# Summing a normalised input's squares on GpSimd, between the weight splits, instead of on VectorE

## The reference

```python
def rms_norm(x, g):
    xf = x.astype(jnp.float32)
    y = xf * lax.rsqrt(jnp.mean(xf * xf, axis=-1, keepdims=True) + EPS)
    return (y * g.astype(jnp.float32)).astype(x.dtype)
...
        y = swiglu_2(rms_norm(x, ffn1_pre_g[l]), ffn1_w_gate[l], ffn1_w_up[l], ffn1_w_down[l])
        x = x + 0.5 * rms_norm(y, ffn1_post_g[l])
        y = hybrid_mixer(rms_norm(x, mix_pre_g[l]), w_in[l], cmp_pe[l], cmp_w1[l], cmp_w2[l],
                         nsa_out_g[l], ret_gn_g[l], w_out[l])
        x = x + rms_norm(y, mix_post_g[l])
```

## Time and profile before

| | |
|---|---|
| median of 3 runs (range) | 3390.71 us (3387.91 to 3391.46) |
| profiled execution | 3393.15 us, of which 3391.7 us span |
| mean granted TensorE clock | 0.985 of full speed |
| busy share PE / DVE / ACT / Pool | 97% / 38% / 37% / 40% |

### The profile page before, as it was taken

The page is one execution under the profiler, slowest core; times in us unless marked ns, Lnnn a source line. Parts: engine busy times, 40 slices in busy tenths (PEclk is TensorE's granted clock), DMA queues, the critical chain, the costliest instruction groups (busy, mean ns, idle before and its releaser), DMA issues.

```text
span 3391.7 us, 45793 instructions
## 1 busy us (share of the span) xinstructions
PE 3281.8 (97%) x17988; PEld 2783.1 (82%) x17988; DVE 1297.6 (38%) x2495; ACT 1242.9 (37%) x2333; POOL 1357.5 (40%) x897
## 2 busy tenths in 40 slices
PE   8999999999999999999999999999999999999998
PEld 6887788898888878888788888888977888688887
DVE  5465443215330534544353305331234553344311
ACT  4454332223222344553332223222334554333221
POOL 3452344444444432343244443444342243244442
PEclk9999999999999999999999999999999999999999
DMA  3221232322232231122123222322241122123322
GB/s 139 75 75 44 68 98 95 101 93 88 96 100 91 90 110 51 63 81 71 61 75 100 97 93 73 108 94 99 85 137 51 46 77 78 50 75 100 100 93 69
DMA packets 81236, 287.32 MB, mean 85 GB/s; under 512 B 8960, under 2 KB 11392, under 8 KB 80640
## 3 DMA queue, kind: packets, MB, share of 16 engines
q1 hardware_dynamic: 79584, 278.42, 25.2%
q10 hardware_dynamic: 1440, 5.98, 0.5%
HBM read 282.26 MB, written 2.10 MB: 84 GB/s over the span
## 4 chain that ended last, share of the span: by engine, by line
PE 85%; DVE 8%; ACT 4%; issue 2%; POOL 1%; DMA 1%; ACTq 0%; DVEq 0%; POOLq 0%
PE bank L263 23%; PE bank L265 22%; PE bank L264 22%; PE bank L1260 3%; PE bank L271 2%; PE bank L273 2%; PE bank L272 2%; PE bank L1236 2%; PE bank L1247 2%; ACT hhi L883 2%; DVE hlo L838 2%; DVE tmp L862 1%; POOL wlo L257 1%; DVE x L833 1%; PE bank L2993 1%
## 5 line engine op out<-in xcount | busy, mean ns | idle before, releaser
L257 POOL TENSOR_TENSOR wlo<-raw,whi 128x256 fp32r<-128x256 f32 (+2 forms) x838 | 1301.1, 1569 | 1880.7 <-ACT whi L243 1838.3
L263 PE MATMUL bank<-hhi,whi 128*128 128x512 f32 x2160 | 868.4, 402 | 10.1 <-POOL wlo L257 3.0
L264 PE MATMUL bank<-hlo,whi 128*128 128x512 f32 x2190 | 860.1, 393 | 0.0
L265 PE MATMUL bank<-hhi,wlo 128*128 128x512 f32 x2160 | 849.1, 393 | 0.0
L243 ACT ACTIVATE whi<-raw 128x1024 fp32r<-128x1024 f32 (+1 forms) x528 | 527.4, 1034 | 389.1 <-PE bank L265 299.5
L263 PEld LDWEIGHTS bank<-hhi,whi 128*128 128x128 f32 x2160 | 410.8, 190 | 96.9 <-issue 15.1
L264 PEld LDWEIGHTS bank<-hlo,whi 128*128 128x128 f32 x2190 | 416.6, 190 | 82.8 <-issue 1.0
L265 PEld LDWEIGHTS bank<-hhi,wlo 128*128 128x128 f32 x2160 | 409.9, 190 | 87.9
L263 PE MATMUL bank<-ff_ahi,whi 128*128 128x512 f32 x660 | 256.7, 389 | 0.0
L265 PE MATMUL bank<-ff_ahi,wlo 128*128 128x512 f32 x660 | 256.7, 389 | 0.0
L264 PE MATMUL bank<-ff_alo,whi 128*128 128x512 f32 x630 | 245.1, 389 | 0.0
(11 more groups left out here) (409 smaller groups left out, 5666.7 us busy)
## 6 DMA issues: line engine op xcount, KB each, us to landing
raw<-wstream SPq DMA_DIRECT2D x516, 512.0 KB, 3.7
raw<-wstream SPq DMA_DIRECT2D x20, 256.0 KB, 3.1
x<-xT ACTq DMA_DIRECT2D x4, 512.0 KB, 10.3
xa_v<-memT ACTq DMA_DIRECT2D x2, 1024.0 KB, 4.8
outT<-x SPq DMA_DIRECT2D x4, 512.0 KB, 2.8
consts<-consts ACTq DMA_DIRECT2D x1, 1062.0 KB, 15.3
m_lw<-lru_w ACTq DMA_DIRECT2D x1, 544.0 KB, 3.6
par<-par SPq DMA_DIRECT2D x2, 248.0 KB, 11.3
```

Source lines behind the costliest of these rows:

```text
L257: last = g.tensor_tensor(h.lo[:, o:o + step], h.raw[:, o:o + step], h.hi[:, o:o + step].bitcast(F32), ALU.subtract)
L263: t.matmul(out, l[0], r[0], start=start, stop=False)
L264: t.matmul(out, l[0], r[1], start=False, stop=False)
L265: return t.matmul(out, l[1], r[0], start=False, stop=stop)
```

## The change

Entry.dve loses its loop of seven adds. Entry.pool gets them: three behind the low part of (first + 1, half 1), four behind the low part of (first + 2, half 0), which is in four pieces, and ahead of root.pool. The waits, the order of the adds, the tiles and the operation stay as they are. Nothing changes on ACT, PE or SP.

```diff
@@ Entry.dve
-        acc = k.tmp[2]
-        for n in range(1, KT):
-            v.wait_ge(*self.sq[n])
-            if n >= 2:
-                v.wait_ge(*self.sq_added[n - 2])
-            v.tensor_tensor(acc[:, :], acc[:, :], self.sq_tile(n)[:, :], ALU.add).then_inc(self.sq_added.sem)
         self.root.dve()
@@ Entry.pool
         weight_lo(self.k, self.first + 1, 1, pieces=4)
+        self.add_squares(1, 4)
         weight_lo(self.k, self.first + 2, 0, pieces=4)
+        self.add_squares(4, KT)
         self.root.pool()
+
+    def add_squares(self, n0, n1):
+        g, acc = self.k.nc.gpsimd, self.k.tmp[2]
+        for n in range(n0, n1):
+            g.wait_ge(*self.sq[n])
+            if n >= 2:
+                g.wait_ge(*self.sq_added[n - 2])
+            g.tensor_tensor(acc[:, :], acc[:, :], self.sq_tile(n)[:, :], ALU.add).then_inc(self.sq_added.sem)
```

## The result

| | median of the runs | lowest to highest | ratio to before (95%) |
|---|---|---|---|
| before | 3389.68 us (4 runs) | 3387.91 to 3391.46 | |
| after | 3420.34 us (4 runs) | 3417.03 to 3423.57 | 1.009 (1.0073 to 1.0108) |

The change makes the kernel 30.7 us slower. The forecast was 3422 us, with a range of 3406 to 3432. The profiled execution took 3418.72 us with a span of 3417.1 us, 25.4 us above the profiled one of before.

What follows compares the result with a forecast made beforehand. PE, busy 97% of the span, bounds the kernel, so its waits for the adds count. Seven "post" Entries 27.3, the "final" 2.4 and clock 1.5 sum to 31.2 us: 3422 us predicted, range 3406 to 3432.

Steps and rivals of the forecast that it cites:

- The add on Pool: One 128x512 add on Pool: 1.27 us, with 0.1 between adds a pitch of 1.37; bounds 0.72 and 1.45.
- The gain of the pieces: Pool's four low-part pieces, without DVE's adds in between, take 2.8 us instead of 4.16, a gain of 1.4 us.
- DVE's delay d: Pool's first three adds hold up DVE's chain in the second half of the tokens: 2.0 us, bounds 0 and 3.6.
- Per "post" Entry: PE's restart after the adds: 1.9 + 2.0 = 3.9 us later, seven times, 27.3 us.
- The "final" Entry: The eighth Entry: Pool's adds end at 780.8, 2.4 us later than PE comes; DVE's delay is hidden there.
- Behind the restart: Order after the last add moves as a whole; only PE's clock may change, 1.5 us for two Entries.
- the sum: All terms for the whole kernel: 27.3 + 2.4 + 1.5 = 31.2 us slower.
- A (no contention): Rival: Pool's first three adds cost DVE nothing; 15.7 us slower, or 3406 us; chance 0.12.
- B (heavier contention): Rival: DVE's delay near 3.6 us, or pitch 1.5, and clock low in each Entry; 44 us, 3435; chance 0.13.
- its third part: The heavier-contention rival's claim that PE's clock is low in each Entry, 3 us of its 44.
- C (a cheap add): Rival: adds cheap on Pool, so the chain's end stays or comes earlier; 3387 us; faster 0.03, no change 0.04.
- D: Rival: PE doesn't wait longer, because its wait is for something other than the adds; chance 0.01.

Runs made afterwards that it cites:

- the first try: Kernel before (adds on DVE), PE's means four steps into the third chunk, row ten in, Pool's second low part ahead of root.pool: 3393.68 us, ratio 1.0014.

## Why the prediction was right

**The add on Pool.** Taken as 1.27 us from the slope of two widths; measured 1.267 in the median. The four of the tail with their gaps: 5.4 us forecast, 5.47 measured.

**The gain of the pieces.** 2.8 us forecast, 2.81 measured.

**DVE's delay d.** 0.4, 1.5 and 2.0 us forecast after each Pool add; 0.4 after the first (low ends at 1143.14 instead of 1139.33 + 3.41), 1.48 after the second and 1.85 at the pieces. Where it costs is made plain by the two kernels with the parts apart. With the first three adds on Pool alone it costs nothing, since four adds are left behind it on DVE instead of seven; it counts where Pool's longer tail stands behind it.

**Per "post" Entry.** 3.9 us forecast, 3.8 measured in the Entry shown, as 6.21 - 4.15 = 2.06 us more waiting at line 396 and 1.75 us of a longer second half. In five of the other six it is 3.8 as well; in the one whose wait had been 4.5 it is 3.4.

**The "final" Entry.** 2.4 us forecast; PE's wait there is 2.42 us, and its restart moves by 2.6 us from where the two kernels stood ahead of the Entry.

**Behind the restart.** 1.5 us had been set aside for the clock in two Entries. It was mis-sized: by ACT's copy of the row behind each restart, the eight Entries lose 5.8 us there. The two that had been named lose the most, 1.8 and 1.5 us, but four others lose 0.5 to 0.8 each. The last Entry, before and after:

```profile
3031.86 1.05 PE L396 MATMUL bank<-consts,tmp 128*128 128x1 f32 x8 [4.15 <-DVE tmp L862]
3038.98 0.60 ACT L897 ACTIVATE row<-bank 128x512 f32<-128x512 f32 x1 [8.29 <-PE bank L730]
```

```profile
3055.84 1.86 PE L396 MATMUL bank<-consts,tmp 128*128 128x1 f32 x8 [6.21 <-POOL tmp L910]
3064.45 0.60 ACT L891 ACTIVATE row<-bank 128x512 f32<-128x512 f32 x1 [11.28 <-PE bank L730]
```

The restart is 23.98 us later and the row 25.47. In the Entry at 1120 us the clock was back at full 5.8 us after the restart before the change, and here PE restarts at 1160.41 and is at the lower level, 1.2 GHz, until 1168, 7.6 us:

```profile
1167.00:1168.00 1.00, 1.00 (x4) 0.81 (x3) 0.00 (x0) 0.00 (x0) 0.00 (x0) 0.50 0.78 254
1168.00:1169.00 1.00, 1.00 (x9) 0.92 (x8) 0.00 (x0) 0.00 (x0) 0.00 (x0) 0.98 0.59 197
```

Before, the next stretch behind the one in the earlier trace rows was already at full clock:

```profile
1159.00:1160.00 1.00, 1.00 (x6) 0.82 (x5) 0.00 (x0) 0.00 (x0) 0.00 (x0) 1.00 0.19 57
```

**What the sum left out.** The eight restarts add up to 28.8 us (29.7 forecast), and with the 5.8 behind them to 34.6. Yet the profiled executions differ by only 25.4. Outside the Entries 1.7 us are lost between the last two, and some 11 us are given back in the two mixers, 3.9 and 7.3. A part of it shows in a wait that has nothing to do with the adds, before and after:

```profile
PE bank L263 <- DVE xa_mlo L2674: 5.0, 2, 2.5
```

```profile
PE bank L263 <- DVE xa_mlo L2678: 1.9, 2, 1.0
```

Before the change PE arrives there early, stands 2.5 us and then runs at half clock for some microseconds (0.50 in the stretch from 1398 to 1402 us). In the profiled execution after, PE had already been slowed a little (0.84 and 0.73 granted from 1394 to 1402), came later, stood 1.0 us and kept its clock. The kernel before also had one wait of 2.5 us for a weight's high part that the changed one hadn't.

The kernels with the last four or with all seven adds behind the pieces, with two adds short and with the adds in halves show the full 5.0 us of the mixers' wait again; the one with the first three on Pool shows 3.5. So it doesn't follow the adds. Whether it belongs to this one execution or to the changed kernel stays open: its four runs all have the same mean clock, 0.983, but only one has a trace. What sets the moment when the clock falls stays open too.

So the mechanism and the Entries' part were forecast well, but that the sum, 31.2 us, lies so near the 30.7 of the medians is partly luck. It had too little behind the restarts and nothing given back in the mixers. By the two profiled executions it was 5.8 us too much; the one of before had been 3.5 us above the median of its runs.

**A reading that was off.** Behind the restart the prediction calls the row at 1158.91 PE's fifth step. It is the fourth; the fifth, the first to need the low part that ends at 1158.69, begins at 1159.66. There was 1 us to spare instead of 0.2, which changes no term.

**The rivals.** A (no contention) fell with the held-up rows of DVE. B (heavier contention) fell too: d is 1.85, not 3.6, and the adds' pitch is no more than forecast. Only its third part, a clock that is low for longer, came in part, with the 5.8 us. C (a cheap add) fell with 1.267 us. D fell with the experiment that shortens two adds: the wait follows the adds one for one.

## What to carry to other kernels

Work that is moved off an engine is priced where the consumer waits for its end: here DVE's 6.9 us were idle time for DVE, but the last of four Pool adds of 1.27 us ended on the path of PE. Before moving such work, ask whether the consumer must wait at that place at all; letting PE begin the next chunk gave 29 us where moving the adds took 31. And when a wait is pushed back, look at what it makes late, and at what stands behind that in every in-order stream: the first try gained nothing, with a row that came later and ACT's next weights queued behind it; with the row early and the low part in pieces, the same ACT order gained 26 us.

## What the runs showed of the hardware

A DVE instruction with two SBUF inputs (0.42 us alone) took up to 1.51 us beside a 128x512 Pool add and up to 0.95 us beside 128x256 ones, while one that reads one of its inputs from PSUM kept 0.47 us. That halving Pool's instructions shortened the longest delay but hardly the sum (1.58 against 1.85 us of DVE's chain) was not expected. Nor was it that PE's clock came back 5.8 us after a restart in one kernel and 7.6 us after it in another, at the same place in the program.
